# A transformer block's up projection as seven block products per tile pair, with the work around it rearranged

## What is computed

```python
x = x + rmsnorm(merged @ w_mix_out, ln_post_mix)          # the "mix", 1024 x 1024 weights
h = rmsnorm(x, ln_pre_ffn)
u = causal_dwconv(h @ w_ffn_up, conv_w, conv_b)           # 1024 x 5632 weights, 3 taps along the rows
u_val, u_gate = split(u, 2)
f = gelu(u_gate) * u_val                                  # 2816 columns
x = x + rmsnorm(f @ w_ffn_down, ln_post_ffn)              # 2816 x 1024 weights
```

## Time and profile before

| | us |
|---|---|
| median of 3 runs | 2445.68 |
| the profiled execution | 2449.56 |
| its span, first to last instruction | 2447.3 |
| PE busy | 2395.4 (98%) |
| POOL busy | 1260.4 (52%) |
| DVE busy | 824.7 (34%) |
| ACT busy | 423.8 (17%) |

### The profile page before, as it was taken

One profiled execution on the slowest core, in us unless ns is written; L12 is line 12 of the kernel. 1 busy time (PEld: TensorE's weight loads), 2 busy tenths in 40 slices (PEclk: granted clock), 3 DMA queues, 4 the chain that ended last, 5 costly groups with the idle time before them and its releaser, 6 DMA issues.

```text
span 2447.3 us, 27437 instructions
## 1 busy us (share of the span) xinstructions
PE 2395.4 (98%) x10702; PEld 1929.4 (79%) x10702; DVE 824.7 (34%) x962; ACT 423.8 (17%) x646; POOL 1260.4 (52%) x684
## 2 busy tenths in 40 slices
PE   8999999999999999999999999999999999999987
PEld 7888788888888888666666888878888888888776
DVE  3000050000177777333334443335332232331423
ACT  4000021110122222111112211023211111111201
POOL 4334333433465555766654468843444343357764
PEclk9999999999999999999999999999999999999999
DMA  5323322226223332654446656643221222244433
GB/s 184 103 86 97 101 77 96 95 94 220 86 78 108 108 112 87 189 153 136 146 142 197 203 196 227 213 155 121 78 69 69 77 70 75 76 155 142 129 123 147
DMA packets 175155, 307.06 MB, mean 125 GB/s; under 512 B 12242, under 2 KB 90322, under 8 KB 175075
## 3 DMA queue, kind: packets, MB, share of 16 engines
q1 hardware_dynamic: 174930, 305.91, 37.9%
q10 hardware_dynamic: 144, 0.07, 0.0%
HBM read 215.75 MB, written 90.18 MB: 125 GB/s over the span
## 4 chain that ended last, share of the span: by engine, by line
PE 70%; issue 15%; POOL 10%; DVE 3%; DMA 1%; ACT 1%; POOLq 0%; SPq 0%; ACTq 0%; DVEq 0%
PE psum L344 19%; PE psum L346 19%; PE psum L345 19%; POOL w_hi L378 5%; POOL w_lo L381 3%; PE psum L1125 2%; PE psum L1409 2%; PE psum L1419 2%; PE psum L1406 1%; DMA d_raw<-ffn_scratch 1%; PE psum L1110 1%; PE psum L1108 1%; DVE d_out L2031 1%; PE psum L1428 1%; PE psum L1393 1%
## 5 line engine op out<-in xcount | busy, mean ns | idle before, releaser
L344 PE MATMUL psum<-act_hi,w_hi 128*128 128x512 f32 x2128 | 853.5, 401 | 0.3 <-issue 0.3
L346 PE MATMUL psum<-act_hi,w_lo 128*128 128x512 f32 x2128 | 831.8, 391 | 0.0
L345 PE MATMUL psum<-act_lo,w_hi 128*128 128x512 f32 x2128 | 829.6, 390 | 0.0
L378 POOL TENSOR_TENSOR w_hi<-w_raw,zero_col 128x1024 fp32r<-128x1024 f32 x181 | 349.8, 1933 | 822.6 <-PE psum L346 813.4
L345 PEld LDWEIGHTS psum<-act_lo,w_hi 128*128 128x128 f32 x2128 | 400.8, 188 | 88.4 <-issue 7.2
L344 PEld LDWEIGHTS psum<-act_hi,w_hi 128*128 128x128 f32 x2128 | 400.6, 188 | 88.5 <-issue 7.6
L346 PEld LDWEIGHTS psum<-act_hi,w_lo 128*128 128x128 f32 x2128 | 400.1, 188 | 86.6
L381 POOL TENSOR_TENSOR w_lo<-w_raw,w_hi 128x1024 fp32r<-128x1024 f32 x181 | 449.4, 2483 | 14.2
L907 POOL TENSOR_TENSOR k_lev<-e_t,g_x 128x896 f32<-128x896 f32 x32 | 96.2, 3007 | 143.6 <-ACT e_t L861 117.1
L344 PE MATMUL psum<-w_hi,act_hi 128*128 128x512 f32 x416 | 162.9, 392 | 1.9 <-POOL w_lo L381 1.6
L345 PE MATMUL psum<-w_lo,act_hi 128*128 128x512 f32 x416 | 162.6, 391 | 0.0
(11 more groups left out here) (178 smaller groups left out, 2549.1 us busy)
## 6 DMA issues: line engine op xcount, KB each, us to landing
w_raw<-in_w_stream SPq DMA_DIRECT2D x225, 512.0 KB, 3.7
proj_scratch<-stage SPq DMA_DIRECT2D x32, 512.0 KB, 2.6
proj_scratch<-side_out SPq DMA_DIRECT2D x64, 256.0 KB, 3.4
r_x<-proj_scratch SPq DMA_DIRECT2D x64, 256.0 KB, 3.3
value_scratch<-stage SPq DMA_DIRECT2D x24, 512.0 KB, 4.8
ffn_scratch<-u_fb SPq DMA_DIRECT2D x22, 512.0 KB, 2.9
d_raw<-ffn_scratch SPq DMA_DIRECT2D x44, 256.0 KB, 3.8
r_v<-value_scratch SPq DMA_DIRECT2D x32, 256.0 KB, 3.2
```

The source lines that it names most:

```text
L344: nc.tensor.matmul(o, s_hi, m_hi, start=start, stop=False)
L345: nc.tensor.matmul(o, s_hi, m_lo, start=False, stop=False)
L346: return nc.tensor.matmul(o, s_lo, m_hi, start=False, stop=stop)
L378: nc.gpsimd.tensor_tensor(w_hi[:, j, :], w_raw[:, j, :], zero_col[:, :].to_broadcast((P, D)), ALU.add).then_inc(sem["hi_split"], 1)
```

## The change

**Up projection.** The rows of h are cut in two halves (512 rows), its inner dimension in two (512), and a pair's weights in four blocks of 512 x 128: B11, B21 (value columns) and B12, B22 (gate columns). With A11, A12 for the first half of the rows and A21, A22 for the second, sums of A are made once, S1 = A21 + A22, S2 = S1 - A11, S3 = A11 - A21, S4 = A12 - S2, and for every pair sums of B: B12 - B11, B22 - (B12 - B11), B22 - B12, B21 - (B22 - (B12 - B11)). Seven products of 4 pieces x 3 matmuls, numbered 1 to 7, follow in one PSUM bank each, and the four result blocks are sums of them: products 1 and 2 give the first half of the value columns, products 1, 6, 7 and 4 the second, products 1, 6, 5 and 3 the first half of the gate columns, products 1, 6, 7 and 5 the second.

**Who does what.** GpSimd makes the weight sums (`sums`, `last_sum`, 128 x 512 each) and the low parts (`lo`); ScalarE rounds the high parts (`up_hi`) and copies product 1 out of PSUM (`up_s1`); VectorE adds up the products from PSUM into SBUF tiles u_cg and u_cv (`s16`, `s167`, `c21`, `add_5`, `up_c11`, `c12`; 7 operations of 128 x 512 a pair). The convolution then reads these SBUF tiles instead of PSUM. Weights are split 8 products ahead at most, half a ring slot each. Pair p's convolution runs beside pair p+2's products. Nothing is a hardware loop any more in this stage.

**Head.** The mix evicts the normed rows once, as raw values (ScalarE), and splits the first two groups (A11, A12) in 1024-wide operations. Pairs 0 to 3 start with products 1 and 2, which need only these; the sums of A, their rounding and their low parts are put in between on ScalarE and VectorE during and after the last group's norm. Two weight slabs (pairs 2 and 3) are loaded to a tile of their own, u_x, behind the last group's residual rows. The barrier ahead of the up projection goes.

**Tail.** SP loads the first four pieces when the last weights are split; ScalarE and VectorE split pieces 0 to 3 ahead of the last pair's last sum, and pieces 4 to 7 one by one between the last convolutions. ScalarE issues the stores of f for pairs 20 and 21. A barrier (`begin_phase(4)`) on SP now stands after the up projection, ahead of the norm weights, the residual rows and pieces 8 and up.

The core of the diff (the tiles' places in memory, the helpers' waits and the renaming of semaphores are left out):

```diff
             mix_hi(act, 1)
-            for g in range(MG):
+            for g in range(MG - 1):
                 squares(g)
                 if g + 2 < MG:
                     mix_hi(act, g + 2)
                 norm_squares(g)
-                evict_hi(g)
+                evict_raw(g)
+                if g < 2:
+                    half_1_hi(g)
+            g = MG - 1
+            squares(g)
+            up_s1(act, 0)
+            norm_squares(g)
+            up_s1(act, 1)
+            a22_hi(2)
+            up_hi(act, 8)
+            evict_raw(g)
+            up_s1(act, 2)
+            block_hi(5, s1_hi[:, :, :], s1_f[:, :, :])
+            up_hi(act, 9)
+            up_s1(act, 3)
+            up_hi(act, 10)
+            block_hi(6, s2_hi[:, :, :], s2_f[:, :, :])
+            up_hi(act, 11)
+            up_hi(act, 12)
+            block_hi(7, s3_hi[:, :, :], s3_f[:, :, :])
+            a22_hi(3)
+            up_hi(act, 13)
+            up_hi(act, 14)
+            up_hi(act, 15)
+            act.wait_ge(sem["act_lo_done"], 2 * KT + 9)
+            block_hi(8, S4_HI, A12_F)
...
                 if g + 2 < MG:
                     mix_lo(dve, g + 2)
+                if g == MG - 1:
+                    sum_1(2)
                 scale(g)
-                evict_lo(g)
+                if g < 2:
+                    half_1_lo(g)
+            up_c11(dve, 0)
+            sum_3(2)
+            up_c11(dve, 1)
+            sum_2(2)
+            sum_4(2)
+            sum_1(3)
+            sum_2(3)
+            dve.wait_ge(sem["s_sum"], 6)
+            block_lo(6, s1_lo[:, :, :], s1_f[:, :, :], s1_hi[:, :, :])
+            sum_3(3)
+            dve.wait_ge(sem["s_sum"], 7)
+            block_lo(7, A11_RAW, s2_f[:, :, :], s2_hi[:, :, :])
+            sum_4(3)
+            block_lo(8, s3_lo[:, :, :], s3_f[:, :, :], s3_hi[:, :, :])
+            up_c11(dve, 2)
+            up_c11(dve, 3)
+            dve.wait_ge(sem["s_sum"], 8)
+            dve.wait_ge(sem["act_lo_done"], 2 * KT + 7)
+            for g, raw in ((2, raw_2), (3, raw_3)):
+                dve.wait_ge(sem["s_hi"], 5 if g == 2 else 9)
+                nc.vector.tensor_tensor(a22_lo[:, :, block_cols(g)], raw[:, 4:8, :],
+                                        A22_HI[:, :, block_cols(g)].bitcast(F32), ALU.subtract
+                                        ).then_inc(sem["act_lo_done"], 1)
+            block_lo(10, A12_RAW, A12_F, S4_HI)
...
+        UP_PRODS = [(0, 1), (1, 1), (0, 2), (1, 2), (2, 1), (3, 1), (2, 2), (3, 2)]
+        UP_PRODS += [(p, i) for i in (5, 6, 7, 4, 3) for p in (0, 1)]
+        UP_PRODS += [(p, i) for p in (2, 3) for i in (6, 7, 4, 5, 3)]
+        UP_PRODS += [(p, i) for p in range(4, FT) for i in (1, 6, 7, 4, 5, 2, 3)]
...
+        def early_slabs(sp):
+            sp.wait_ge(sem["m_mm"], 6)
+            for p in (2, 3):
+                sp.dma_start(u_x[:, p - 2, :], w_stream[UP_STREAM + 2 * p, :, :]).then_inc(sem["u_x_in"], 16)
...
+            def sums(p):
+                wait_raw(pool, p, 0)
+                wait_raw(pool, p, 1)
+                t1, t2 = u_t[:, p % 2, 0, :], u_t[:, p % 2, 1, :]
+                if p < 2:
+                    pool.wait_ge(sem["m_mm"], 6)
+                else:
+                    pool.wait_ge(sem["u_lo"], max(prod_index(p - 2, 5), prod_index(p - 2, 4)) + 1)
+                nc.gpsimd.tensor_tensor(t1, raw_half(p, 1, 0), raw_half(p, 0, 0), ALU.subtract
+                                        ).then_inc(sem["u_sum"], 1)
+                pool.wait_ge(sem["u_sum"], sum_count(p, 1))
+                nc.gpsimd.tensor_tensor(t2, raw_half(p, 1, 1), t1, ALU.subtract).then_inc(sem["u_sum"], 1)
+                nc.gpsimd.tensor_tensor(raw_half(p, 1, 0), raw_half(p, 1, 1), raw_half(p, 1, 0), ALU.subtract
+                                        ).then_inc(sem["u_sum"], 1)
+            def last_sum(p):
+                pool.wait_ge(sem["u_lo"], prod_index(p, 6) + 1)
+                pool.wait_ge(sem["u_sum"], sum_count(p, 3))
+                t2 = u_t[:, p % 2, 1, :]
+                nc.gpsimd.tensor_tensor(t2, raw_half(p, 0, 1), t2, ALU.subtract).then_inc(sem["u_sum"], 1)
+            def lo(p, i):
+                n = prod_index(p, i)
+                pool.wait_ge(sem["u_hi"], n - 7)
+                nc.gpsimd.tensor_tensor(w_lo8[:, n % 8, :], block_raw(p, i), w_hi8[:, n % 8, :].bitcast(F32),
+                                        ALU.subtract).then_inc(sem["u_lo"], 1)
...
+        def up_hi(act, n):
+            if n >= N_PROD:
+                return
+            p, i = UP_PRODS[n]
+            if i in (1, 2):
+                wait_raw(act, p, 0)
+            elif i == 3:
+                wait_raw(act, p, 1)
+            else:
+                act.wait_ge(sem["u_sum"], sum_count(p, {5: 1, 6: 2, 7: 3, 4: 4}[i]))
+            act.wait_ge(sem["u_prod"], n - 7)
+            nc.scalar.activation(w_hi8[:, n % 8, :], block_raw(p, i), ACT.Copy).then_inc(sem["u_hi"], 1)
...
+            for n in range(16, 26):
+                up_hi(act, n)
+            for p in range(2, FT):
+                lin_g(p - 2)
+                lin_v(p - 2)
+                if p >= 4:
+                    up_s1(act, p)
+                    up_hi(act, prod_index(p, 1) + 8)
+                up_hi(act, prod_index(p, 6) + 8)
+                gelu(p - 2)
+                up_hi(act, prod_index(p, 7) + 8)
+                up_hi(act, prod_index(p, 4) + 8)
+                up_hi(act, prod_index(p, 5) + 8)
+                if p < 4:
+                    early_c11(p)
+                else:
+                    up_hi(act, prod_index(p, 2) + 8)
+                up_hi(act, prod_index(p, 3) + 8)
+            for k in range(RING):
+                split_hi(act, k, 0, k, True)
+            lin_g(FT - 2)
+            lin_v(FT - 2)
+            gelu(FT - 2)
+            f_store(act, FT - 2)
+            lin_g(FT - 1)
+            lin_v(FT - 1)
+            split_hi(act, RING, 1, 0, False)
+            gelu(FT - 1)
+            split_hi(act, RING + 1, 1, 1, False)
+            split_hi(act, RING + 2, 1, 2, False)
+            f_store(act, FT - 1)
+            split_hi(act, RING + 3, 1, 3, False)
...
+            for p in range(2, FT):
+                taps(p - 2, 1)
+                s16(p)
+                taps(p - 2, 0)
+                f(p - 2)
+                s167(p)
+                c21(p)
+                add_5(p)
+                if p >= 4:
+                    up_c11(dve, p)
+                if p < FT - 1:
+                    c12(p)
+            for k in range(RING):
+                split_lo(dve, k, k, True)
+            c12(FT - 1)
+            taps(FT - 2, 1)
+            taps(FT - 2, 0)
+            f(FT - 2)
+            taps(FT - 1, 1)
+            split_lo(dve, RING, 0, False)
+            taps(FT - 1, 0)
+            split_lo(dve, RING + 1, 1, False)
+            f(FT - 1)
+            split_lo(dve, RING + 2, 2, False)
+            split_lo(dve, RING + 3, 3, False)
...
+            def product(n):
+                p, i = UP_PRODS[n]
+                hi, lo = {1: (A11_HI, A11_LO), 2: (A12_HI, A12_LO), 3: (S4_HI, A12_RAW), 4: (A22_HI, a22_lo),
+                          5: (s1_hi, s1_lo), 6: (s2_hi, A11_RAW), 7: (s3_hi, s3_lo)}[i]
+                pe.wait_ge(sem["u_lo"], n + 1)
+                if p < 4:
+                    pe.wait_ge(sem["act_lo_done"], 2 * KT + {1: 4, 2: 4, 5: 5, 6: 6, 7: 7, 4: 9, 3: 10}[i])
+                if n < 4:
+                    pe.wait_ge(sem["act_hi_done"], 2 * KT + 3 * KT)
+                elif n < 8:
+                    wait_evicted(pe, *UP_PRODS[n - 4])
+                elif n < 12:
+                    pe.wait_ge(sem["act_hi_done"], 2 * KT + 4 * KT)
                 else:
-                    pe.wait_ge(sem["d_res"], NT)
-                half_product((SL_UP + k) % RING, k, 0)
-            first_half(0)
-            first_half(1)
+                    wait_evicted(pe, *UP_PRODS[n - 8])
+                for k in range(4):
+                    cols = slice(k * P, (k + 1) * P)
+                    last = product3(prod_bank(n), w_hi8[:, n % 8, cols], w_lo8[:, n % 8, cols],
+                                    hi[:, k, :], lo[:, k, :], k == 0, k == 3)
+                last.then_inc(sem["u_prod"], 1)
+            for n in range(4):
+                product(n)
             mix_transposes(pe, MG - 1)
-            end_phase(pe, "pe")
-            first_half(2)
-            first_half(3)
-            pe.wait_ge(sem["act_lo_done"], 2 * KT + 4 * KT)
-            for k in range(RING):
-                half_product((SL_UP + k) % RING, k, 1).then_inc(sem["mm_half"], 2)
-            def body(k, n, grp, j, early):
-                pe.wait_ge(sem["u_tap0"], k + 1)
-                slab_product(pe, n, j, (j - SL_UP) % RING)
-            repeat(pe, SL_UP + RING, 2 * FT - RING, body)
+            for n in range(4, N_PROD):
+                product(n)
```

573 lines of the change are left out of this document (414 added, 159 removed).

## The result

| | before | after | ratio, 95% interval |
|---|---|---|---|
| median, us | 2445.12 | 2412.11 | 0.9866 (0.9848 to 0.9883) |
| median, second session, us | 2446.66 | 2413.82 | 0.987 (0.9855 to 0.9886) |
| profiled execution, us | 2449.56 | 2415.3 (span 2413.5) | |

The account below looks back on a forecast made before the run. The prediction took TensorE's plain count of matmuls to bound the up projection. From the 2445.68 us median, -59.9 for fewer matmuls, +10 head, +10 tail and +1 clock (-38.9) gave 2407 us, range 2391 to 2434.

Parts of the forecast that it names:

- Part 1: Up projection: 264 fewer matmuls at 0.2269 us each, -59.9 us; a pair takes 19.06 us.
- the bound of 14.6: Up projection: +14.6 us if the seven products ran at the down stage's step; 0 was taken.
- Part 2: Engines behind TensorE in the up projection: GpSimd almost full at 18.4 of 19.06 us a pair; cost taken 0.
- rival C: Up projection: GpSimd takes over the beat at 20.2 us a pair, 2427 us (2418 to 2440); chance 0.18.
- Part 3: Head of the up projection: TensorE stalls of 2, 2, 4 and 2.5 us, together +10 us (4 to 20).
- Part 4: Tail into the down stage: stalls of 4, 2.5 and 3.5 us, together +10 us (1 to 17).
- slab 5: Tail: piece 5 comes 34.5 us after the last product, wanted at 32.1: stall 2.5 us (0 to 6).
- A: Whole kernel: the count bounds the stage and the seams cost 13 to 30 us, 2397 to 2418 us; chance 0.58.
- B: Seams: VectorE's waits fall in GpSimd's gaps, under 13 us in all, 2387 to 2397 us; chance 0.15.
- D: Up projection: GpSimd's 512-wide two-input form costs much more, 2495 us at 1.7 us an operation; chance 0.07.
- E: Up projection: unrolled products run the old count, gain gone and seams remain, 2467 us; chance next to nothing.
- C's second road: Up projection: a wider step between matmuls would end in the same place, 2421 us; within the chance of 0.18.

Follow-up runs that it names:

- e1_cross: Changed kernel with moving operands crossed from pair 4 on (products 5, 6, 7 take A11 tiles, 1 and 2 those of S1 and S3): 2416.47 us.
- e5_halves: Changed kernel with the stationary operand of pairs 4 to 19 read from two scratch tiles instead of the weight tiles: 2418.12 us.
- e3_extra: Changed kernel with two more 512-wide subtractions on GpSimd in each pair from pair 6 on: 2455.66 us.
- e2_taps: Changed kernel with VectorE's five two-SBUF-input operations of a pair (four taps and the product f) cut to 8 columns: 2404.81 us.
- e12_head: As e9, with the head's activation sum of group 3 for S1 put ahead of group 2's sums for S2 and S4 on VectorE: 2395.09 us.
- e7_tail: Changed kernel with down pieces 8 to 11 issued ahead of barrier and residual, and the last c12 behind the first of four low pieces: 2412.17 us.
- e4_c12: Changed kernel with the last pair's c12 put ahead of VectorE's four low pieces for the down stage: 2416.83 us.
- e9: As e7_tail, plus the half turn's low parts 4 and 5 between output steps and queues behind the last convolutions in the down stage's order: 2396.28 us.
- e11_after: The changed kernel itself, unchanged, run again beside the other runs on the same chip: 2413.82 us.

## Why the prediction was right, and where it was off

The time lies 5.1 us over the forecast and the mechanism is the one forecast, but that the miss is so small is in part luck: terms of +6.8 and +2.7 us were missing, and the tail was 3.8 us too dear.

**Part 1, the count.** Right: 264 matmuls at 0.2269. The step that failed is the one that took 0 for the new operands' place. Its argument was that the form stays, and the row that spoke against it, 0.2348 in the down stage, was kept as a bound only. A pair takes 19.38 us instead of 19.06, 0.2306 a matmul; over 1848 matmuls that is +6.8 us, about half of the bound of 14.6. e1_cross and e5_halves show that it goes with the tiles: four of seven products (6 and 4 with one of their two moving tiles) pair weights with a moving tile on the other side of SBUF. Its size is measured, not explained. This mis-sized term is larger than the whole miss of 5.1.

**Part 2, the engines behind.** Right, and the narrow margin was real: 18.7 us by after and by e3_extra against 18.4, TensorE at 19.4. e2_taps shows that it costs nothing in mid-stage, e3_extra that it would have from half an operation more. The Trainium skill, "SBUF — State Buffer", "Who interferes with whom", was weighed here: the pair of engines it names is the right one, and operations with one input in PSUM stayed at 0.68 us as it says; but an operation of 1.2 to 1.3 us cost the other engine 0.87 to 0.98. By whole lengths a pair of after would be the 20.2 us of rival C, and e3_extra's 22.8, where it was 21.3.

**Part 3, the head.** 9.6 us of waits where 10 were forecast: transposes 1.4 (2), product 8 3.0 (2), product 16 0.8 (4), bank waits 1.1 (2.5); not foreseen were 2.0 at product 12 and 1.2 at 1804.9, both on GpSimd's low parts. Two of the four terms were well over and 3.2 us came from places the forecast did not name, so the sum is nearer than its parts were. What speaks for more than luck is that the cause was right: VectorE and GpSimd take turns there, and e12_head moved the single waits while the stage stayed as long. A further 2.7 us lies around the waits: a step that holds one is 0.16 us longer than the wait and a plain step together (eight of them, 1.3 us), and 16 steps of 0.29 to 0.35 us follow them or lie between 1780 and 1825 (1.4 us). There GpSimd was just in time at best: its low part for product 1 ended 0.05 us ahead of TensorE in each of pairs 4, 5 and 6, so up to 1825 us rival C's mechanism was at work in small. No step of the sum had these 2.7 us (6.8 + 9.6 + 2.7 - 0.26 of issue before = 18.8, where the stage kept 18.7 of the 59.9).

**Part 4, the tail.** 7.2 us instead of 10 + 1: c12 3.2 (4), slab 5 none (2.5), slab 8 2.6 (3.5), clock 1.6 (1). The places were right and each a little cheaper. That slab 5 was in time because the c12 wait itself let VectorE run the taps alone is what e7_tail suggests. The forecast added three waits that stand one behind the other; e4_c12 and e7_tail show that such waits replace each other, at least in part.

**Rivals.** A came true, 6 us inside the upper end of its 2397 to 2418 (by the sum's own numbers that range is seams of 11 to 32 us, not 13 to 30). B wanted seams under 13 us; they cost 16.8 (9.6 + 7.2). C, D and E did not come true; C's second road, the wider step, was half right. The total was 5.1 us over the forecast, and the terms make 5.3: +6.8 of spacing, +2.7 of slow restarts, -3.8 in the tail, -0.4 in the head's waits.

## What to carry to other kernels

When a rewrite removes matmuls, read the step between matmuls per operand pair, and if a row with one operand elsewhere in SBUF is slower, charge it. Where two engines slow each other, price their work by turns, and take the sum of a contended stretch rather than its single waits. At a seam, order each queue by when its reader wants the piece, and issue early loads ahead of barriers and large ones: at the seam into the down stage and at its half turn together that was worth 15.9 us here, half of what the change itself gave. The half turn's 7.7 to 8.8 us of it were to be had in the kernel before as well.

## What the runs showed of the hardware

- **Two sides of SBUF.** A stream of 128x512 matmuls steps at 0.2267 us when stationary and moving tile lie both among the activation and weight tiles (up to byte 131199 of the partition, as e5_halves' expectation gives it) or, as e5_halves suggests, both in the scratch tiles above 132800. When they lie on different sides it steps at 0.2290 or at 0.2333; the same tiles did either, and what chooses is open. It comes down to 0.2267 within about one product of 12. The Trainium skill, "SBUF — State Buffer", "Who interferes with whom", says that TensorE's two read ports are independent and that it never waits on another engine. e2_taps agrees with the second (843 matmuls with and without VectorE's operations). No run here shows whether the first bears on the 1 to 3% that the placement costs.
- **The clock behind a wait** (all waits of TensorE of 1.4 us or more between 1700 and 2320 us in the changed kernel's two profiles and in those of e1 to e9 and e12): at 2.02 us and less it stayed at 1.00 every time; at 3.2 us and more it fell to the lower level every time, with 7 to 14 steps of 0.43 us, 1.6 to 2.9 us lost; between 2.58 and 3.07 us it went either way, staying behind product 8 after 3.03 us in the first profile of after and falling after 3.07 us in e11_after. So a wait of 3 us is priced at 3 us or at 5 to 6.
- **A drop can cost nothing.** The 2.9 us that the clock took in e11_after (14 steps of 0.43 us) came off the next two waits, 2.02 to 0.37 us and 0.84 to none, since GpSimd was the limit there; the stage was no longer (439.9 us against 440.3).
